# Gate and up of a mixture-of-experts block as one product of 512 columns, with the three combining sums and the copy of h moved

## The reference, cut to what matters

```python
def expert_block(args):
    xe, e = args
    gt = jnp.minimum(xe @ w_gate[e] + b_gate[e], SWIGLU_LIMIT)
    up = jnp.clip(xe @ w_up[e] + b_up[e], -SWIGLU_LIMIT, SWIGLU_LIMIT)
    h = gt * jax.nn.sigmoid(SWIGLU_ALPHA * gt) * (up + 1.0)
    return h @ w_down[e] + b_down[e]
# each token's four results are weighted by its router shares and added
```

## Time and profile before

| | |
|---|---|
| median of 3 runs | 1459.44 us (1458.39 to 1459.88) |
| the profiled execution | 1456.15 us, its span 1454.4 us |
| PE busy | 1358.7 us, 93% of the span |
| DVE busy | 583.3 us, 40% |
| ACT busy | 269.9 us, 19% |
| DMA | 458.63 MB, 315 GB/s over the span |
| gate and up products (line 1299), busy | 432.6 us, 7424 records, 385 ns each |
| down product (line 1367), busy | 214.2 us, 3712 records, 381 ns each |

### The profile page before, as it was taken

One profiled execution on the slowest core, in us unless ns is written; L12 is line 12 of the kernel. 1 busy time (PEld: TensorE's weight loads), 2 busy tenths in 40 slices (PEclk: granted clock), 3 DMA queues, 4 the chain that ended last, 5 costly groups with the idle time before them and its releaser, 6 DMA issues.

```text
span 1454.4 us, 41463 instructions
## 1 busy us (share of the span) xinstructions
PE 1358.7 (93%) x17038; PEld 766.0 (53%) x17039; DVE 583.3 (40%) x1111; ACT 269.9 (19%) x563; POOL 112.8 (8%) x327
## 2 busy tenths in 40 slices
PE   7999999999969999999999999999898998869994
PEld 5777674576544455555555555555454544335552
DVE  1069994451174333333333333333332333223335
ACT  0111113241111121112111211121111111111122
POOL 3400000000001100010000100100000000000100
PEclk9999999999978999999999999999999999999997
DMA  8333233516778970697997997999999999999991
GB/s 246 122 137 136 95 138 114 181 59 264 283 332 355 428 315 0 285 427 328 423 426 323 426 424 322 428 427 425 426 425 428 427 427 424 428 426 426 425 424 58
DMA packets 63026, 458.63 MB, mean 315 GB/s; under 512 B 4370, under 2 KB 7042, under 8 KB 30203
## 3 DMA queue, kind: packets, MB, share of 16 engines
q1 hardware_dynamic: 62714, 457.98, 76.8%
q10 hardware_dynamic: 289, 0.33, 0.1%
HBM read 454.09 MB, written 4.73 MB: 315 GB/s over the span
## 4 chain that ended last, share of the span: by engine, by line
PE 75%; DMA 18%; DVE 3%; SPq 2%; issue 1%; ACT 1%; ACTq 0%; DVEq 0%
PE PS L1299 21%; DMA SB<-in_w_down_dram 17%; PE PS L1025 14%; PE PS L1367 12%; PE PS L1322 6%; PE PS L1280 5%; PE PS L1005 3%; PE PS L1177 2%; PE PS L1118 2%; PE PS L1073 2%; PE PS L1197 2%; SPq L240 2%; PE PS L1305 1%; PE PS L1309 1%; DMA SB<-in_w_in_dram 1%
## 5 line engine op out<-in xcount | busy, mean ns | idle before, releaser
L1299 PE MATMUL PS<-SB 128*32 128x256 f32 x7424 | 432.6, 385 | 38.9 <-DMA SB<-in_w_up_dram 22.3
L1299 PEld LDWEIGHTS PS<-SB 128*32 128x32 f32 x7424 | 236.7, 111 | 217.4 <-issue 55.6
L922 DVE SCALAR_TENSOR_TENSOR SB<-PS,SB 128x1024 f32<-128x1024 f32 x177 | 194.9, 1101 | 83.1 <-PE PS L1322 83.1
L1367 PE MATMUL PS<-SB 128*32 128x256 f32 x3712 | 214.2, 381 | 7.3 <-DMA SB<-in_w_down_dram 7.3
L1025 PE MATMUL PS<-SB 128*128 128x320 f32 x768 | 209.2, 435 | 4.2 <-DMA SB<-in_w_in_dram 4.2
L1025 PEld LDWEIGHTS PS<-SB 128*128 128x128 f32 x768 | 146.8, 191 | 65.4 <-issue 5.5
L932 DVE TENSOR_SCALAR PS<-PS 128x256 f32<-128x256 f32 x58 | 25.1, 432 | 380.7 <-PE PS L1309 380.7
L1367 PEld LDWEIGHTS PS<-SB 128*32 128x32 f32 x3712 | 113.7, 110 | 89.7 <-DMA SB<-in_w_down_dram 11.9
L1322 PE MATMUL PS<-SB 32*128 32x256 f32 (+1 forms) x1416 | 124.8, 422 | 4.0 <-DVE SB L922 3.4
L669 DVE SCALAR_TENSOR_TENSOR SB<-SB 128x350 f32<-128x350 f32 x240 | 118.6, 572 | 0.0
L1280 PE MATMUL PS<-SB 128*32 128x256 f32 (+1 forms) x1416 | 98.1, 391 | 0.0
(11 more groups left out here) (214 smaller groups left out, 893.8 us busy)
## 6 DMA issues: line engine op xcount, KB each, us to landing
SB<-in_w_gate_dram SPq DMA_DIRECT2D x64, 2048.0 KB, 27.3
SB<-in_w_up_dram SPq DMA_DIRECT2D x64, 2048.0 KB, 32.6
SB<-in_w_down_dram SPq DMA_DIRECT2D x64, 2048.0 KB, 34.6
SB<-in_w_in_dram SPq DMA_DIRECT2D x14, 2048.0 KB, 8.0
SB<-in_w_pw_dram SPq DMA_DIRECT2D x2, 2048.0 KB, 9.9
SB<-in_w_att_o_dram SPq DMA_DIRECT2D x2, 2048.0 KB, 7.9
SB<-in_w_out_dram SPq DMA_DIRECT2D x2, 2048.0 KB, 8.2
SB<-rev_bias SPq DMA_DIRECT2D x2, 1024.0 KB, 8.4
```

The costliest lines, as they stand in the source:

```text
L922: dve.scalar_tensor_tensor(y, ps, gcol[:, tt:tt + 1], y, ALU.mult, ALU.add).then_inc(sem("yadd"), 1)
L1299: ins = pe.matmul(PS[32 * q:32 * q + 32, bank, 0:256], xg[:, c % 2, c // 2, :], buf[:, c, 256 * q:256 * q + 256], start=(c == 0), stop=False)
L1367: ins = pe.matmul(PS[32 * n:32 * n + 32, 2, 256:512], hT[:, ck % 2, ck // 2, :], WD[par][:, ck, 256 * n:256 * n + 256], start=(ck == 0), s ...
```

## The change

Gate and up of one parity now lie in buffers at one fixed distance, so that a view `WGU` reads both, and one product of 2 x 256 = 512 columns per chunk and quarter makes both, into the whole of PSUM bank 0. Its bias is one set of 8 products of 512 columns. Nothing stands between the chunks of this product. Sum 0 stands behind it, ahead of the gather; the broadcast is one product of 320 columns, ahead of the turn of h; sum 1 stands behind the turn of h, sum 2 in the middle of the down product. On DVE, min of gate now writes `tin`, the clamp of up follows at once, then the addition of sum 0, then the product with the sigmoid (now in `sg`, the space of `hT`), h, and the copy of the turned h, which ACT did before. The turn of x goes to bank 0. SP waits for `gu_half` and `gu_read` and loads gate 0, up 0, gate 1, up 1, down 0, down 1; the last, `gu_read`, is given before the bias. The first loads go to the same places in the same order, under new names.

```diff
-        WG, WU, WD = (wbuf[2], wbuf[0]), (wbuf[1], wbuf[5]), (wbuf[4], wbuf[3])
+        WG, WU, WD = (wbuf[1], wbuf[0]), (wbuf[2], wbuf[3]), (wbuf[4], wbuf[5])
+        every = SB[:, 0:6 * WB].rearrange("p (m c n) -> p m c n", m=6, c=KC)
+        WGU = every[:, 1:3], every[:, 0:4:3]
...
+        sg = view(M0 + 512, 256)
...
-                    load_halves(sp, WG[par], weights(wg_v, e), f"wg{par}", ["gate_half", "gate_done"], used)
-                    load_halves(sp, WU[par], weights(wu_v, e), f"wu{par}", ["up_half", "up_done"], used)
-                    load_halves(sp, WD[par], weights(wd_v, e), f"wd{par}", ["down_half", "down_done"], used)
+                    for h, read in enumerate(("gu_half", "gu_read")):
+                        sp.wait_ge(sem(read), used)
+                        load_half(sp, h, WG[par], weights(wg_v, e), f"wg{par}")
+                        load_half(sp, h, WU[par], weights(wu_v, e), f"wu{par}")
+                    for h, read in enumerate(("down_half", "down_done")):
+                        sp.wait_ge(sem(read), used)
+                        load_half(sp, h, WD[par], weights(wd_v, e), f"wd{par}")
...
                 act.wait_ge(sem("gmin"), i + 1)
-                act.wait_ge(sem("trx_mm"), i + 1)
-                act.activation(tin, PS[:, 0, 0:256], ACT.Sigmoid, scale=SW_ALPHA).then_inc(sem("sig"), 1)
+                act.activation(sg, tin, ACT.Sigmoid, scale=SW_ALPHA).then_inc(sem("sig"), 1)
                 act.wait_ge(sem("trh_mm"), i + 1)
-                act.copy(hT, PS[:, 3, 0:256].rearrange("p (j q s) -> p j q s", j=2, q=Q)).then_inc(sem("hT_ready"), 1)
...
-                    dve.wait_ge(sem("gate_done"), i + 1)
-                    dve.tensor_scalar(PS[:, 0, 0:256], PS[:, 0, 0:256], LIMIT, None, ALU.min).then_inc(sem("gmin"), 1)
+                    dve.wait_ge(sem("gu_done"), i + 1)
+                    dve.tensor_scalar(tin, PS[:, 0, 0:256], LIMIT, None, ALU.min).then_inc(sem("gmin"), 1)
+                    dve.tensor_scalar(PS[:, 0, 256:512], PS[:, 0, 256:512], LIMIT, -LIMIT, ALU.min, ALU.max).then_inc(sem("upc"), 1)
+                    add_tile(i, 0)
                     dve.wait_ge(sem("sig"), i + 1)
-                    dve.tensor_tensor(tin, tin, PS[:, 0, 0:256], ALU.mult).then_inc(sem("gsig"), 1)
-
-                    add_tile(i, 0)
-
-                    dve.wait_ge(sem("up_done"), i + 1)
-                    dve.tensor_scalar(PS[:, 1, 0:256], PS[:, 1, 0:256], LIMIT, -LIMIT, ALU.min, ALU.max).then_inc(sem("upc"), 1)
+                    dve.tensor_tensor(tin, tin, sg, ALU.mult).then_inc(sem("gsig"), 1)
+                    dve.wait_ge(sem("upc"), i + 1)
                     dve.wait_ge(sem("gsig"), i + 2)
-                    dve.wait_ge(sem("upc"), i + 1)
-                    dve.scalar_tensor_tensor(tin, PS[:, 1, 0:256], 1.0, tin, ALU.add, ALU.mult).then_inc(sem("h_ready"), 1)
-
+                    dve.scalar_tensor_tensor(tin, PS[:, 0, 256:512], 1.0, tin, ALU.add, ALU.mult).then_inc(sem("h_ready"), 1)
+
+                    dve.wait_ge(sem("trh_mm"), i + 1)
+                    dve.tensor_copy(hT, PS[:, 3, 0:256].rearrange("p (j q s) -> p j q s", j=2, q=Q)).then_inc(sem("hT_ready"), 1)
                     add_tile(i, 1)
                     add_tile(i, 2)
...
+            def gate_up(par, c):
+
+                for q in range(Q):
+                    ins = pe.matmul(PS[32 * q:32 * q + 32, 0, :].rearrange("p (w n) -> p w n", w=2), xg[:, c % 2, c // 2, :],
+                                    WGU[par][:, :, c, 256 * q:256 * q + 256], start=(c == 0), stop=False)
+                return ins
...
                         pe.wait_ge(sem("xg_ready"), i + 1)
-                        pe.wait_ge(sem("gsig"), i + 1)
+                        for c in range(KC):
+                            if c % 4 == 0:
+                                pe.wait_ge(sem(f"wg{par}_{c // 4}"), q * 16 + 16)
+                                pe.wait_ge(sem(f"wu{par}_{c // 4}"), q * 16 + 16)
+                            if c == KC - 1:
+                                pe.wait_ge(sem("hot_ready"), i * 2 + 2)
+                            ins = gate_up(par, c)
+                            if c == 3:
+                                ins.then_inc(sem("gu_half"), 1)
+                            if c == KC - 1:
+                                ins.then_inc(sem("gu_read"), 1)
+                        gate_up_bias()
+                        pe.wait_ge(sem("y_sb"), i + 1)
                         pe.wait_ge(sem("scat_ready"), i + 1)
-                        gate_or_up(0, WG[par], f"wg{par}", q * 16 + 16, 0, "gate_half", "gate_done", i * 2 + 2)
-                        pe.wait_ge(sem("y_sb"), i + 1)
                         combine(i, 0)
-                        pe.wait_ge(sem("h_ready"), i + 1)
-                        gate_or_up(1, WU[par], f"wu{par}", q * 16 + 16, 1, "up_half", "up_done")
-                        combine(i, 1)
                         pe.wait_ge(sem("sel_ready"), i + 3)
                         pe.wait_ge(sem("tin_x"), i + 1)
                         gather(sel)
 
-                        pe.wait_ge(sem("hT_ready"), i + 1)
+                        who = hot16[:, 0:1].broadcast_to([E, P])
+                        pe.matmul(PS[:, 1, 0:T], who, rankT, start=True, stop=True).then_inc(sem("bc_mm"), 1)
+
                         pe.wait_ge(sem("h_ready"), i + 2)
                         for j in range(2):
                             ins = tr(PS[:, 3, P * j:P * j + P], tin[:, j:256:2])
                         ins.then_inc(sem("trh_mm"), 1)
-
-                        who = hot16[:, 0:1].broadcast_to([E, P])
-                        pe.matmul(PS[:, 0, 256:512], who, rankT[:, 0:256], start=True, stop=True)
-                        pe.matmul(PS[:, 1, 256:256 + NS_], who, rankT[:, 256:T], start=True, stop=True).then_inc(sem("bc_mm"), 1)
-                        combine(i, 2)
+                        combine(i, 1)
                         turn_x(i + 2)
...
                             if ck == KC // 2 - 1:
                                 ins.then_inc(sem("down_half"), 1)
+                                combine(i, 2)
```

More of the change, by code:

```diff
@@ L232, in apart, with load_half @@
             eng.wait_ge(sem("tables_done"), 1)
-        def load_halves(eng, buf, src, name, used=None, count=None):
+        def load_half(eng, h, buf, src, name):
             step = src.shape[1] // 2
[L237 to L240, removed]
+            eng.dma_start(buf[:, 4 * h:4 * h + 4, :], src[:, step * h:step * h + step, :]).then_inc(sem(f"{name}_{h}"), 16)
         def weights(v, e):
@@ L313, in _ @@
             sp.wait_ge(sem("p_mm"), PAIRS)
-            load_halves(sp, WG[0], wg_v[0], "wg0")
+            for h in range(2):
+                load_half(sp, h, WU[0], wu_v[0], "wu0")
             sp.wait_ge(sem("o_mm"), PAIRS)
@@ L582, in turned @@
             def turned():
-                act.copy(xg, PS[:, 3, 256:512].rearrange("p (j q s) -> p j q s", j=2, q=Q)).then_inc(sem("xg_ready"), 1)
+                act.copy(xg, PS[:, 0, 0:256].rearrange("p (j q s) -> p j q s", j=2, q=Q)).then_inc(sem("xg_ready"), 1)
             act.wait_ge(sem("gath_mm"), 2)
@@ L952, in _ @@
                     dve.wait_ge(sem("tables_done"), 1)
[L953 to L955 removed]
+                    dve.tensor_scalar(scat, PS[:, 1, 0:T], slotcol[:, bass.ds(b, 1)], None, ALU.is_equal).then_inc(sem("scat_ready"), 1)
                     dve.wait_ge(sem("gcol_set"), i + 1)
@@ L1287, in turn_x @@
                 for j in range(2):
-                    ins = tr(PS[:, 3, 256 + P * j:256 + P * j + P], tin[:, P * j:P * j + P])
+                    ins = tr(PS[:, 0, P * j:P * j + P], tin[:, P * j:P * j + P])
                 ins.then_inc(sem("trx_mm"), 1)
-            def gate_or_up(bank, buf, loaded, count, which, half, done, hot_count=None):
-                for c in range(KC):
-                    if c % 4 == 0:
-                        pe.wait_ge(sem(f"{loaded}_{c // 4}"), count)
-                    if c == 4 and hot_count is not None:
-                        pe.wait_ge(sem("hot_ready"), hot_count)
-                    for q in range(Q):
-                        ins = pe.matmul(PS[32 * q:32 * q + 32, bank, 0:256], xg[:, c % 2, c // 2, :],
-                                        buf[:, c, 256 * q:256 * q + 256], start=(c == 0), stop=False)
-                    if c == KC // 2 - 1:
-                        ins.then_inc(sem(half), 1)
+            def gate_up(par, c):
[3 more added lines that the diff above has]
+                return ins
@@ L1303, in gate_or_up, with gate_up_bias @@
+            def gate_up_bias():
                 for q in range(Q):
                     r = slice(64 * (q // 2), 64 * (q // 2) + 64)
-                    pe.matmul(PS[32 * q:32 * q + 32, bank, 0:256], hot[r, 0:1].broadcast_to([64, SLOTS]), bias_hm[r, which, q % 2, :],
-                              start=False, stop=False)
```

(8 more changed lines are left out.)

18 lines of the change are left out of this document (11 added, 7 removed).

## The result

The changed kernel takes 1482.43 us, the median of four runs (1479.32 to 1484.14), against 1459.48 of the kernel before on the same chip: 1.0156 times as long, with an interval of 1.0138 to 1.0174, 22.9 us. The profiled execution took 1482.95 us, its span is 1480.9. The forecast was 1478.6 in a range of 1459 to 1491, slower with 0.80.

The account below looks back on a forecast made before the run. PE was taken to bound up to the 13th expert's last block, the weight stream through the 28th expert, then PE; 8.1, 5.9, 1.7, 1.1 and 2.4 sum to 19.2 us over 1459.44, giving 1478.6, range 1459 to 1491.

Parts of the forecast that it names:

- The parts of the block: PE's own work in one block, summed from the earlier trace's starts: 15.72 us, of it product 6.98 and bias 0.65.
- the rival that put 0.41 on a change of tile shape: Faster rival: two removed shape changes give 0.41 us each, not 0.11; block 14.9, time 1445 us; chance 0.10.
- h's chain: DVE's work from first bias group to h: 3.71 us against PE's 3.11, so PE waits 0.60 before turning h.
- the start of a pair: Extra PE time where a pair of experts starts: put at 0.5 us each (0.48 at 1318.66).
- The release: A weight buffer comes free after half the joint product, 3.43 us instead of 1.72; holes end 1.7 us later.
- start and landing of 2.3: Weight stream from the issue at 884.51: 2.3 us beyond 84 pieces of 4.92 us each.
- a rival at up to 1.7: Much slower rival (1489 us, chance 0.12): PE's clock falls behind waits; the last, on the path, adds up to 1.7.
- 27 blocks on PE: Blocks up to the 13th expert's last, where PE sets the time: 0.3 us more each, 8.1 us.
- waits of four long experts: Second up half late at experts 4, 7, 10 and 13: 9.4 us less 3.5 of existing waits, 5.9.
- order within the 28th expert: Second up half lands 9.84 us before down 1; the expert ends 3.0 after it instead of 1.93: 1.1.
- 8 blocks at the end: Last blocks, after the stream's stretch, where PE sets the time again: 8 x 0.3 = 2.4 us.
- the prediction's own factor: Each 0.1 us of block time is worth 2.4 us in total, since longer blocks also shorten waits.

Follow-up runs that it names:

- before: The kernel without the change: 1459.48 us on the same chip as the changed kernel's runs.
- after: The changed kernel, with gate and up as one joint product, against the kernel before it: 1482.43 us, 1.0156 times as long.
- x2_need: The kernel before, with loads in the new order and the gate product waiting for both matrices' half: 1483.8 us, ratio 1.0169.
- x8_gather: The kernel before, with the gather between gate product and bias, turn of x ahead of that of h, sum 2 behind: 1472.41 us, ratio 1.0101.
- x1_split: The changed kernel with gate and up as two 256-column products, loaded and released in the old order: 1465.6 us, ratio 1.0045 to the kernel before.

## Why the prediction held, and where its steps were off

The parts of the block. Product 6.98 (said 6.98), bias 0.65 (0.65), sum 0 0.65, gather 1.57, turn of h 0.44, the down product from its start to the next joint product 4.20 with sum 2 inside (the sum had 3.85 less a turn of 0.37, plus 0.59 and 0.10: 4.17). The bias of two groups at 0.325 each agrees with the 0.11 that the sum took from rows, and so does PE's own work in the block, 16.20 - 0.46 = 15.74 where the sum had 15.72; the rival that put 0.41 on a change of tile shape is out. The Trainium skill says (TensorEngine Tiling (Array Packing), Key Properties) that a change of tiling mode drains the engine; the trace agrees, at 0.11.

The step that was off is h's chain, and with it the block: 16.3 said, 16.20 measured. From the first bias group DVE starts after 559.13 - 558.35 = 0.78, as said. The last product starts 561.44 - 560.99 - 0.41 = 0.04 behind the one it depends on, where I had taken 0.11 from a hand-over in the earlier trace rows, and PE follows 561.92 - 561.86 = 0.06 behind it: 3.57 in place of 3.71. The wait is 3.57 less 3.11 of PE's work, 0.46, where 0.60 stood (the 0.40 that the trace calls idle begins only where the broadcast product ends). 0.1 a block is 2.4 us too much: 3.5 in the two lines on blocks below, less 1.1 that shorter blocks add to the waits.

The weight stream. Second up half late at the first block of the 4th, 7th, 10th and 13th expert, said as 3.5, 1.8, 2.3 and 1.8: from the starts of the joint products around them, less 16.20 for a block and 0.67 for the start of a pair, they cost 5.6, 2.1, 2.7 and 2.0, together 12.4 against 9.4 (by the same reckoning the waits of before were 2.9, said as 3.5). Of that 9.9 are the idle times shown above and 1.7 the clock; the rest is what PE takes to run on behind each wait. Against the sum, 1.7 is the clock and 1.1 the shorter block, which arrives earlier; the start of a pair was 0.67 in the differences of both kernels and 0.5 in my sum, which works the other way. The release is 1.9 late (1.7 said). From the issue at 905.53 to 1311.56 it is 406.0; start and landing of 2.3 and 82 pieces of 4.92 make 405.7, so the stream's pace was right.

The end. Behind 1311.56 the joint product's second half takes 6.41 instead of 3.64: 2.8 us at half clock on the path to the end. I had it in a rival at up to 1.7, and not in the forecast.

The whole, from the first product of the loop to the last of the down products, is 989.6 us in the trace before and 1012.3 in that after. The spans of these two executions differ by 26.5, since the loop starts 4.0 us later in the second, at 445.95 instead of 441.98, behind a part that the change leaves alone; over all ten traces it starts at 441.98 to 446.18, with both kinds of kernel at either end.

The difference, by parts:

| | said | measured |
|---|---|---|
| 27 blocks on PE | 8.1 | 5.4 |
| waits of four long experts | 5.9 | 9.5, of it clock 1.7 |
| release | 1.7 | 1.9 |
| order within the 28th expert | 1.1 | 1.0 |
| 8 blocks at the end | 2.4 | 1.6 |
| clock at the end | (rival) | 2.8 |
| first block, rest | | 0.5 |
| sum | 19.2 | 22.7 |

22.7 against 22.9 between the medians. So the mechanisms were right and two sizes were not, in opposite directions: the block too dear by 3.5 with the end's share, waits and clock too cheap by 6.4. That they partly cancel is luck: it is why the forecast is 3.5 us off and not more. The experiments bear the split out from three sides. Taking the joint product apart leaves 6.1, against 24 x 0.24 = 5.8 by the prediction's own factor. The need alone costs 24 in the kernel before, but with clock losses in more places than after has, so it shows the mechanism and not its share. And halving the pieces gives 12 to 14 back at an unchanged block.

What stays open: the price of the half clock is read from rows and was not tested by itself, and no trace row names 0.3 of the 0.5 in the row "first block, rest". The later release was read from the traces alone; no run has it without the earlier need.

## What to carry to other kernels

When two products are merged, ask first what lies between them now and whom it covers; here the addition of sum 0 and the gate half of h's work on DVE ran under the up product, and merging saved 0.26 us of PE work a block (16.00 less 15.74) and laid 0.46 of waiting bare. Then ask when the merged product needs its operands and when it frees them: where transfers just keep up, needing the fourth piece 3.4 us into a block instead of 6.4 cost, with the release 1.9 later, some 16 us here, more than 0.26 a block can give back. Halving the pieces made up for 12 to 14 of the 23 us, though not for all, and in the kernel before, where little was lost on it, it gained nothing. Price a new wait of some 2 us or more with the half clock that can follow it, not by its length alone.

## What the runs showed of the hardware that I had not expected

With a wait of PE on weights the granted clock can fall to 1.2 GHz, during the wait or when PE works again. In x2_need at the 4th expert it is full from 499 to 500 us and 0.50 from 501 to 503, all inside the wait; in after it is still full at 504.00 to 504.50, where the wait ends, and 0.61 from 504.50 to 506. At the long experts it fell with waits of 2.39, 2.83 and everything from 2.95 up, and not with 1.79, 1.86, 2.47, 2.49 and, at the 16th expert of after, 2.61; a wait of 2.39 did it and longer ones did not. Where the stream sets the pace the picture is as mixed: in x8_gather it stayed full behind 2.73, 2.77 and 2.87, in x1_split it fell behind 2.21 and 1.99 (2.66 and 2.54 us for 1.93, at 1027.65 and 1116.27), and before has such losses too (2.64 for 1.93 behind a wait of 2.87, at 1024.54). So the length of the wait alone doesn't decide. At the long experts and the 28th it cost 1.4 to 2.8 us each time. The Trainium skill (TensorE: Matmul & The Clock Gate, HAM oscillation) describes a kernel whose waits on transfers throttle PE again and again. These traces agree, with those prices.

Pieces of 1 MB ran at 422 GB/s where pieces of 2 MB ran at 426. Two DVE operations of which the second needs the first's result started 0.04 us apart from end to start, less than I had read from the kernel before; and a product of 512 columns was worth next to nothing against two of 256 straight behind each other (0.04 us a block).
